# Splitting first loads, seams and the last norm of an encoder layer kernel, and holding GpSimd's sums back

## The chip, the cores and the metric

The kernel runs on one core of one Trainium2 chip. The metric is device time in microseconds (us) of one launch. The core's engines are TensorE (PE; weight loads are shown as PEld), VectorE (DVE), ScalarE (ACT), GpSimd (POOL) and SyncE (SP), which issues the DMA transfers. They run side by side and wait for each other through counting semaphores.

## What is computed

One encoder layer in float32, width D = 1024, for 1024 + 256 = 1280 tokens (two sequences, laid side by side), in these steps:

```
z      = x @ w_in                                    # 1024 wide, into heads, rwkv parts, gates
o_att  = attention(q, k, v)                          # 8 query heads, 2 key/value heads
o_rw   = (groupnorm(wkv scan both ways) + bonus) * g # 16 heads of 64
merged = gate0 * (o_rw @ w_proj_rwkv) + gate1 * (o_att @ w_proj_attn)
h      = layernorm(ALPHA * x + merged @ w_out)       # over the 1024 columns
ff     = square(relu(h @ w_ff1)) @ w_ff2             # 4096 wide
y      = layernorm(ALPHA * h + ff)
```

## The kernel before

Activations are kept transposed: 8 tiles of 128 rows (columns of the model), each with 1280 tokens along the free dimension. Six stages follow each other, with a barrier of all engines between them (class `Stage`): attention, scaled, gate, state, merge, tail. Inside a stage each engine has its own written-out list of instructions, and only semaphores order them across engines. The change touches three places.

*Attention stage, start.* SP first loads the weights of head 0 (512 KB), then the eight tiles of x (640 KB each), then the rest. TensorE's `head(0)` runs k outermost: for each of eight tiles k it multiplies spans of 512, 512 and 256 tokens into three PSUM banks, so that it can start with the first tile. A float32 matmul appears as two passes of weight load and product.

*Merge stage.* It has 16 blocks i, of 24 products each. Blocks 0 to 7 multiply the attention output (in xT); blocks 8 to 15 multiply the recurrent output oR. During blocks 0 to 7 the group norm of oR is done beside: ACT squares, TensorE sums over heads, ACT takes Ln and Exp, DVE scales, adds the bonus and multiplies by the gate g, one step of `normed` for each tile i and span j, 24 in all. Block 8 waits for all 24 on TensorE. `gating` on DVE multiplies a block's result by its gate (semaphore `gated`) and from block 8 adds it to merged (`added`), in one operation each over 1280 tokens. SP reloads xT with x when block 7 is done, and the weights of block 9 follow it in the queue.

*Tail stage.* The tokens are in two halves (H = 640), each of two quarters (Q = 320). Products come in pairs n, each a seven-product scheme in place of eight: sums of weight blocks (DVE, `add_weights`, semaphore `s_done`) times sums of token blocks. For the out projection the token sums of half 0 are DVE's (`wide_sums`, `tm_done`), those of half 1 GpSimd's (`other_half`, `tn_done`), both at the start of the stage; those of half 1 are first used by pair 4. A pair's products raise z1 to z7, and DVE's gathers out of PSUM raise e1 to e7. `p1(n+1)` is the first product of the next pair.

Each of the four norms (two layer norms, two halves; the last is N2H1) runs in steps: GpSimd adds the eight rows of 640 tokens (`totals`, four calls p = 0 to 3, the last two adds behind the last pair), TensorE multiplies the total by ones (means), DVE subtracts (`centre`), ACT squares, the squares are summed, TensorE multiplies by ones (variance), ACT takes Ln and Exp (`root`), a multiply by rstd (`scale`), ACT's `affine` (gain and bias), SP stores. For N2H1 TensorE sums the squares of all eight rows itself (16 products), and DVE scales all eight rows.

## Time and profile before

| | us |
|---|---|
| median of 3 runs | 3328.92 (3327.21 to 3331.74) |
| the profiled execution | 3333.99 |
| its span | 3332.2 |
| TensorE busy in it | 3216.5 (97%) |
| DVE, ACT, GpSimd busy | 1787.0, 1040.4, 136.9 |
| GpSimd's four sums at the start of the tail stage | 2176.05 to 2190.9 |
| last product of the last pair ends | 3297.4 |

The span runs from the first to the last recorded instruction; times in rows are from its start. Busy time adds the durations of an engine's instructions. Matmuls are pipelined and their ends are modelled, so a busy TensorE is not one at its peak. In a row, the bracket holds the engine's idle time before it and what ended it.

### The profile page before, as it was taken

What the parts mean: (1) busy time and instruction counts of PE and PEld (TensorE: products, weight loads), DVE (VectorE), ACT (ScalarE), POOL (GpSimd) and SP (SyncE); (2) the same over time, 40 slices, a digit from 0 to 9 for tenths busy, and PEclk for the clock granted to TensorE, in tenths of its full rate; (3) what the DMA queues carried; (4) which work ended last, traced back from release to release, by engine and by line L of the source; (5) the groups of instructions that cost most, each with busy time, mean ns of one, the idle gap of its engine ahead of it and who ended that gap; (6) DMA issues with size and microseconds to landing.
All of it is one profiled execution on the core that took longest, in us unless ns stands there. A gap on an engine that the chain in (4) does not pass through costs nothing. (4 is left out here: it accounts for less than half of the span.)

```text
span 3332.2 us, 59858 instructions
## 1 busy us (share of the span) xinstructions
PE 3216.5 (97%) x25992; PEld 2047.2 (61%) x25992; DVE 1787.0 (54%) x2925; ACT 1040.4 (31%) x1590; POOL 136.9 (4%) x90
## 2 busy tenths in 40 slices
PE   9999999999999999989999999989999999999997
PEld 4564565554555555577787554567666666666665
DVE  2337763677767579056566232155645446545455
ACT  2336652334334124333443452002321111221111
POOL 0000000000000000000000000025200000200001
PEclk9999999999999999999999999999999999999998
DMA  3221111334534424265564223212112112122111
GB/s 139 57 73 33 45 33 49 122 123 148 184 124 129 177 95 151 100 193 167 170 171 126 84 88 140 82 38 76 58 61 75 68 64 82 57 95 82 63 64 57
DMA packets 218534, 328.53 MB, mean 99 GB/s; under 512 B 55456, under 2 KB 176544, under 8 KB 213152
## 3 DMA queue, kind: packets, MB, share of 16 engines
q1 hardware_dynamic: 218272, 324.69, 29.9%
q8 instruction: 207, 3.39, 0.4%
q14 instruction: 55, 0.45, 0.0%
HBM read 221.74 MB, written 96.34 MB: 95 GB/s over the span
## 5 line engine op out<-in xcount | busy, mean ns | idle before, releaser
L641 PE MATMUL ra_ps<-xT,ring 128*128 128x512 f32 (+1 forms) x1152 | 429.8, 526 | 0.0
L1817 PE MATMUL tl_ps<-merged,pool 128*128 128x320 f32 x1440 | 406.1, 434 | 4.6 <-PEq L108 3.9
L1817 PEld LDWEIGHTS tl_ps<-merged,pool 128*128 128x128 f32 x1440 | 274.6, 191 | 121.0 <-issue 7.5
L641 PEld LDWEIGHTS ra_ps<-xT,ring 128*128 128x128 f32 x1152 | 214.5, 190 | 198.8 <-issue 189.1
L2069 DVE TENSOR_TENSOR oR<-tl_ps,oR 128x320 f32<-128x320 f32 x416 | 202.3, 490 | 152.7 <-PE tl_ps L1817 149.9
L1091 PE MATMUL rg_ps<-xT,ring 128*128 128x512 f32 (+1 forms) x720 | 267.5, 527 | 3.3 <-PEq L108 3.3
L1817 PE MATMUL tl_ps<-tl_Th,pool 128*128 128x320 f32 x720 | 205.5, 437 | 6.5 <-DVE xT L2067 6.5
L1902 ACT ACTIVATE ring<-tl_ps 128x320 f32<-128x320 f32 x96 | 42.0, 437 | 533.7 <-PE tl_ps L1817 533.7
L1091 PEld LDWEIGHTS rg_ps<-xT,ring 128*128 128x128 f32 x720 | 135.6, 192 | 115.4 <-issue 109.9
L2075 DVE TENSOR_TENSOR merged<-tl_ps,ring 128x320 f32<-128x320 f32 x96 | 47.2, 492 | 256.0 <-PE tl_ps L1817 140.5
L1817 PE MATMUL tl_ps<-xT,pool 128*128 128x320 f32 x640 | 182.7, 432 | 0.0
L1817 PEld LDWEIGHTS tl_ps<-tl_Th,pool 128*128 128x128 f32 x720 | 138.4, 192 | 64.9 <-issue 9.1
L1817 PE MATMUL tl_ps<-merged,tl_sums 128*128 128x320 f32 x544 | 161.8, 437 | 5.8 <-DVE oR L2067 3.3
L1297 PE MATMUL rc_ps<-pool 64*128 64x192 f32 x1280 | 153.3, 356 | 6.7 <-DVE rc_ps L1498 3.5
L303 PE MATMUL at_ps<-xT,ring 128*128 128x512 f32 (+1 forms) x432 | 159.1, 521 | 0.0
L1817 PEld LDWEIGHTS tl_ps<-xT,pool 128*128 128x128 f32 x640 | 121.7, 190 | 50.6
L1449 DVE TENSOR_TENSOR rc_SC<-rc_ps,cst 128x512 f32<-128x512 f32 x160 | 110.4, 690 | 71.1 <-PE rc_ps L1297 71.1
L1594 PE MATMUL mg_ps<-xT,ring 128*128 128x512 f32 (+1 forms) x384 | 144.5, 530 | 1.9 <-PEq L108 1.9
L328 PE MATMUL at_ps<-at_qk 128*128 128x512 f32 (+1 forms) x288 | 135.8, 594 | 8.3 <-ACT at_p L395 7.9
L1594 PE MATMUL mg_ps<-oR,ring 128*128 128x512 f32 (+1 forms) x384 | 139.4, 526 | 2.9 <-DVE oR L1647 2.9
L340 PE MATMUL at_ps<-at_turned,at_v 32*128 32x256 f32 x2176 | 137.0, 386 | 4.0 <-DVE at_ot L479 4.0
L340 PEld LDWEIGHTS at_ps<-at_turned,at_v 32*128 32x128 f32 x2176 | 108.4, 185 | 49.0 <-issue 43.4
(243 smaller groups left out, 4730.3 us busy)
## 6 DMA issues: line engine op xcount, KB each, us to landing
pool<-ub SPq DMA_DIRECT2D x320, 160.0 KB, 2.8
ub<-ra_ub SPq DMA_DIRECT2D x32, 1280.0 KB, 5.3
pool<-in_w_ff SPq DMA_DIRECT2D x32, 1024.0 KB, 4.8
pool<-in_w_ff SPq DMA_DIRECT2D x64, 512.0 KB, 3.5
ring<-in_w_in SPq DMA_DIRECT2D x39, 512.0 KB, 3.6
xT<-in_xT SPq DMA_DIRECT2D x16, 640.0 KB, 8.2
ub<-ra_v SPq DMA_DIRECT2D x16, 640.0 KB, 6.5
mg_gate<-gates SPq DMA_DIRECT2D x16, 640.0 KB, 3.9
```

The source lines that it names most:

```text
L303: last = pe.matmul(ps[:, z_bank(i) + j, 0:n], w[:, i % 3, 128 * k:128 * k + 128], xT[:, k, t0:t0 + n], start=(k == 0), stop=(k == KT - 1))
L328: last = pe.matmul(ps[:, 2 * (t % 2) + b // 512, 0:n], qk[:, h, t0:t0 + 128], qk[:, QH + h // (QH // KVH), k0 + b:k0 + b + n], start=True, ...
L340: last = pe.matmul(ps[:, 4 + i, 0:256], values_of(g, i, j), pT[g % 2][32 * i:32 * i + 32, j].rearrange("p t q -> p (t q)"), start=(j == 0) ...
L641: last = pe.matmul(ps[:, bank + j, 0:n], w[c][:, 128 * i:128 * i + 128], xT[:, i, t0:t0 + n], start=(i == 0), stop=(i == KT - 1))
L1091: last = pe.matmul(ps[:, 3 * (b % 2) + j, 0:n], w[b % 3][:, 128 * i:128 * i + 128], xT[:, i, t0:t0 + n], start=(i == 0), stop=(i == KT - 1))
L1297: last = pe.matmul(ps[:, 4 + 2 * (q % 2) + h, 192 * j:192 * j + 192], x[rows, 2 * q + j, CH:3 * CH], x[rows, 2 * q + j, 3 * CH:6 * CH], st ...
L1449: dve.tensor_tensor(SC[g % 2][:, 2 * q:2 * q + 2, :, :], score_view(ps, q, 0, 2 * CH), cst[:, at:at + 128].unsqueeze(1).unsqueeze(1).broad ...
L1594: last = pe.matmul(ps[:, 3 * (i % 2) + j, 0:n], w[i % 2][:, 128 * k:128 * k + 128], src[:, k, t0:t0 + n], start=(k == 0), stop=(k == KT - 1))
L1817: last = pe.matmul(bank(n, b), lhs(k), rhs(k), start=(fresh and k == 0), stop=(k == d - 1), skip_group_check=True)
L1902: act.activation(cp[n % 2][:, c, :], bank(n, b), ACT.Copy).then_inc(done, 1)
L2069: dve.tensor_tensor(y, bank(n, b), y, ALU.add).then_inc(done, 1)
L2075: dve.tensor_tensor(hidden(n, i, j), bank(n, b), cp[n % 2][:, c, :], ALU.add).then_inc(done, 1)
```

## The change

Five edits are made. (1) The first weights and the first x tile are loaded in two pieces each, the first 128 columns of w and the first 512 tokens of x first, with a semaphore of their own; TensorE waits for the pieces as it comes to them. (2) Block 8 of the merge waits for the last tile's `normed` steps only before its k = 7 products. (3) The last block's gating runs span by span. (4) GpSimd's `other_half` waits until DVE's four token sums and the weight sums of pairs 0 and 1 are done. (5) In the last norm DVE adds the last two rows to the totals by quarters; the squares are added in pairs of rows, two pairs by GpSimd and two by DVE, so that TensorE has 8 products in place of 16; GpSimd scales rows 6 and 7 and applies gain and bias to them; and the stores go in the order 0, 1, 2, 6, 3, 4, 7, 5.

```diff
@@ attention_stage, SP
-            load(0)
-            for k in range(KT):
+            sp.dma_start(w[:, 0, 0:128], hbm["w_in"][B_Q + HEADS[0]][:, 0:128]).then_inc(first_ready, 16)
+            sp.dma_start(xT[:, 0, 0:512], hbm["xT"][0:128, 0:512]).then_inc(first_ready, 16)
+            sp.dma_start(xT[:, 0, 512:T], hbm["xT"][0:128, 512:T]).then_inc(x_ready[0], 16)
+            sp.dma_start(w[:, 0, 128:D], hbm["w_in"][B_Q + HEADS[0]][:, 128:D]).then_inc(w_ready[0], 16)
+            for k in range(1, KT):
@@ attention_stage, TensorE, head(0)
-                        pe.wait_ge(x_ready[k], 16)
+                        if k == 0:
+                            pe.wait_ge(first_ready, 32)
+                        else:
+                            pe.wait_ge(x_ready[k], 16)
+                        if k == 1:
+                            pe.wait_ge(w_ready[0], 16)
                         for j, (t0, n) in enumerate(SPANS):
+                            if k == 0 and j == 1:
+                                pe.wait_ge(x_ready[0], 16)
@@ merge_stage, TensorE
                 if i == KT:
-                    pe.wait_ge(normed, 3 * KT)
+                    pe.wait_ge(normed, 3 * KT - 3)
...
                     for k in range(KT):
+                        if i == KT and k == KT - 1:
+                            pe.wait_ge(normed, 3 * KT - 2 + j)
...
-                    if j == 2:
+                    if i == 2 * KT - 1:
+                        last.then_inc(z_part, 1)
+                    elif j == 2:
                         last.then_inc(z_ready, 1)
@@ merge_stage, DVE
-            for i in range(KT, 2 * KT):
+            for i in range(KT, 2 * KT - 1):
                 gating(i)
+            i = 2 * KT - 1
+            dve.wait_ge(gate_ready[i % 2], 16 * (i // 2) + 16)
+            for j, (t0, n) in enumerate(SPANS):
+                g, m = gate[i % 2][:, t0:t0 + n], merged[:, KT - 1, t0:t0 + n]
+                dve.wait_ge(z_part, j + 1)
+                dve.tensor_tensor(g, ps[:, 3 * (i % 2) + j, 0:n], g, ALU.mult).then_inc(gated_part, 1)
+                dve.wait_ge(gated_part, j + 1)
+                dve.tensor_tensor(m, m, g, ALU.add).then_inc(added, 1)
@@ tail_stage, SP
-            store(N2H1)
+            for k in (0, 1, 2, 6, 3, 4, 7, 5):
+                if k < 6:
+                    sp.wait_ge(normed, 8 * N2H1 + k + 1)
+                else:
+                    sp.wait_ge(gp_normed, k - 5)
+                sp.dma_start(hbm["y"][128 * k:128 * k + 128, H:T], rows(N2H1, k)).then_inc(stored, 16)
@@ tail_stage, TensorE, variance of N2H1
-            for k in range(KT):
-                pe.wait_ge(sq_done, 8 * N2H1 + k + 1)
+            for k in range(0, KT, 2):
+                pe.wait_ge((gp_sums, dve_sums)[k // 4], k % 4 // 2 + 1)
                 for j in range(2):
...
@@ tail_stage, ACT
-            for k in range(KT):
+            for k in range(6):
                 affine(N2H1, k)
@@ tail_stage, GpSimd
-                    if 0 <= p < 4:
+                    if 0 <= p < (3 if q == N2H1 else 4):
...
+            gp.wait_ge(tm_done, 4)
+            gp.wait_ge(s_done, 8)
             for which in (1, 2, 3, 4):
                 other_half(which)
...
+            for k in (0, 2):
+                gp.wait_ge(sq_done, 8 * N2H1 + k + 2)
+                gp.tensor_tensor(squares(N2H1, k), squares(N2H1, k), squares(N2H1, k + 1), ALU.add).then_inc(gp_sums, 1)
+            gp.wait_ge(r_done, N2H1 + 1)
+            for k in (6, 7):
+                gp.wait_ge(centred, 8 * N2H1 + k + 1)
+                gp.tensor_tensor(rows(N2H1, k), rows(N2H1, k), rstd[:, :], ALU.mult).then_inc(gp_scaled, 1)
+                gp.wait_ge(gp_scaled, k - 5)
+                gp.tensor_scalar(rows(N2H1, k), rows(N2H1, k), glob[:, G_L2G + k:G_L2G + k + 1], glob[:, G_L2B + k:G_L2B + k + 1],
+                                 ALU.mult, ALU.add).then_inc(gp_normed, 1)
@@ tail_stage, DVE
+            def last_total(k, j, ready, done):
+                n, t = PAIRS_N - 1, tot[:, Q * j:Q * j + Q]
+                if k == 3:
+                    dve.wait_ge(tot_part, 6 * N2H1 + 5)
+                else:
+                    dve.wait_ge(end_part, (1, 2)[j])
+                dve.wait_ge(ready, n + 1)
+                dve.tensor_tensor(t, t, rows(N2H1, k)[:, Q * j:Q * j + Q], ALU.add).then_inc(done, 1)
...                                  # behind gather e3 of the last pair
+                if n == PAIRS_N - 1:
+                    last_total(3, 0, e2, end_part)
+                    last_total(3, 1, e3, end_part)
+                    last_total(7, 1, e7, tot_part)
...                                  # behind gather e4
+                if n == PAIRS_N - 1:
+                    dve.wait_ge(tot_part, 6 * N2H1 + 6)
+                    last_total(7, 0, e4, tot_done)
...
             for k in range(KT):
                 centre(N2H1, k)
-            for k in range(KT):
+            for k in (4, 6):
+                dve.wait_ge(sq_done, 8 * N2H1 + k + 2)
+                dve.tensor_tensor(squares(N2H1, k), squares(N2H1, k), squares(N2H1, k + 1), ALU.add).then_inc(dve_sums, 1)
+            for k in range(6):
                 scale(N2H1, k)
```

## Rows read from the trace of the kernel before

**Rows 1.** The page's engine line: busy us (share of the span) xinstructions.

```profile
PE 3216.5 (97%) x25992; PEld 2047.2 (61%) x25992; DVE 1787.0 (54%) x2925; ACT 1040.4 (31%) x1590; POOL 136.9 (4%) x90
```

**Rows 2.** Timeline of the start: start us, us, engine, line, operation [idle before <-releaser].

```profile
6.21 19.21 PE L297 MATMUL at_ps<-xT,ring 128*128 128x512 f32 x48 [6.21 <-DMA xT<-in_xT]
8.90 0.34 PEld L297 LDWEIGHTS at_ps<-xT,ring 128*128 128x128 f32 x1 [0.52 <-issue]
```

**Rows 3.** Timeline of the merge stage, end of block 7 and block 8.

```profile
2029.06 0.70 PE L1578 MATMUL mg_ps<-mg_gd,mg_wg 128*128 128x256 f32 x2 [0.28 <-DVE oR L1647]
...
2032.67 35.66 PE L1594 MATMUL mg_ps<-oR,ring 128*128 128x512 f32 x93 [2.91 <-DVE oR L1647]
...
2051.83 1.49 DVE L1632 TENSOR_TENSOR mg_gate<-mg_ps,mg_gate 128x1280 f32<-128x1280 f32 x1 [17.91 <-PE mg_ps L1594]
```

**Rows 4.** Timeline of the last norm.

```profile
3298.19 3.14 POOL L1992 TENSOR_TENSOR ring<-ring,oR 128x640 f32<-128x640 f32 x2 [3.30 <-DVE oR L2069]
3301.38 2.50 PE L1888 MATMUL tl_ps<-ring,cst 128*128 128x320 f32 x4 [3.94 <-POOL ring L1992]
...
3303.91 5.94 DVE L2079 TENSOR_TENSOR oR<-oR,tl_ps 128x640 f32<-128x640 f32 x8 [5.95 <-PE tl_ps L1888]
3304.77 5.86 ACT L1925 ACTIVATE xT<-oR 128x640 f32<-128x640 f32 x8 [65.82 <-DVE oR L2079]
...
3305.65 11.25 PE L1895 MATMUL tl_ps<-xT,cst 128*128 128x320 f32 x32 [1.77 <-ACT xT L1925]
...
3320.67 6.60 ACT L1930 ACTIVATE oR<-oR,glob 128x640 f32<-128x640 f32 x8 [0.89 <-DVE oR L2083]
```

**Rows 5.** Windows of the last norm: stretch, length, busy us by engine, PEclk, DMA share, GB/s.

```profile
3305.60:3310.50 4.90, 4.85 (x9) 3.21 (x10) 4.25 (x6) 4.90 (x7) 0.00 (x0) 0.50 0.01 3
...
3319.80:3327.30 7.50, 0.00 (x0) 0.00 (x0) 5.97 (x8) 6.60 (x8) 0.00 (x0) 0.56 0.65 260
```

**Rows 6.** Timeline of the attention stage, a shorter stall of TensorE and what follows.

```profile
215.09 0.70 PE L286 MATMUL at_ps<-at_turned,cst 128*128 128x256 f32 x2 [2.47 <-ACT at_turned L372]
...
215.62 6.64 PE L318 MATMUL at_ps<-ring,xT 128*128 128x256 f32 x30
```

**Rows 7.** Windows of the start of the program.

```profile
0.00:3.00 3.00, 0.00 (x0) 0.00 (x0) 0.00 (x0) 0.00 (x0) 0.20 (x4) 1.00 0.28 76
3.00:6.00 3.00, 0.00 (x0) 0.00 (x0) 0.00 (x0) 0.00 (x0) 0.00 (x0) 1.00 1.03 417
```

**Rows 8.** One line in a stretch, 2025 to 2060: weight loads of the merge stage.

```profile
L1543 SPq DMA_DIRECT2D ring<-in_w_merge x2: 328/442/556, 2032.3 to 2051.8; - x2
...
DMA to landing us min/median/max: 3.6/8.0/12.4
```

**Rows 9.** Timeline of the merge stage's end and the tail stage's start.

```profile
2172.14 1.49 DVE L1632 TENSOR_TENSOR mg_gate<-mg_ps,mg_gate 128x1280 f32<-128x1280 f32 x1 [14.17 <-PE mg_ps L1594]
2173.66 1.49 DVE L1634 TENSOR_TENSOR merged<-merged,mg_gate 128x1280 f32<-128x1280 f32 x1
...
2175.98 0.69 DVE L2024 TENSOR_TENSOR pool<-pool 128x512 f32<-128x512 f32 x1 [0.83 <-PEq L108]
...
2176.05 3.37 POOL L1969 TENSOR_TENSOR oR<-merged 128x1280 f32<-128x1280 f32 x1 [754.45 <-POOLq L108]
2176.59 4.18 DVE L2037 TENSOR_TENSOR tl_Th<-merged 128x1280 f32<-128x1280 f32 x1
...
2188.07 0.47 DVE L2067 SCALAR_TENSOR_TENSOR xT<-xT,tl_ps 128x320 f32<-128x320 f32 x1
...
2188.69 9.49 PE L1817 MATMUL tl_ps<-tl_Th,pool 128*128 128x320 f32 x24 [6.46 <-DVE xT L2067]
```

**Rows 10.** Timeline of the tail stage's second pair, DVE and one product of TensorE.

```profile
2201.38 0.69 DVE L2032 TENSOR_TENSOR tl_sums<-pool,tl_sums 128x512 f32<-128x512 f32 x1
...
2209.39 0.68 DVE L2024 TENSOR_TENSOR pool<-pool 128x512 f32<-128x512 f32 x1
...
2215.24 2.32 PE L1817 MATMUL tl_ps<-merged,tl_sums 128*128 128x320 f32 x8
```

**Rows 11.** One line of the program, in the gate stage: GpSimd's copies, duration ns.

```profile
L1141 POOL COPY pool<-cst x2: 609/611/613, 1121.8 to 1122.3; 128x512 f32<-128x512 f32 x2
```

More of the change, by code:

```diff
@@ L173, in attention_stage @@
         w_ready = st.sems("w_ready0 w_ready1 w_ready2")
-        c_ready, tab_ready, om, zr_ready = st.sems("c_ready tab_ready om zr_ready")
+        c_ready, tab_ready, om, zr_ready, first_ready = st.sems("c_ready tab_ready om zr_ready first_ready")
         z_ready, sq_done, zq_done, stat_ready, ln_done, rt_done, zn_done, cos_done, sin_done, head_done = st.sems(
@@ L288, in head @@
             def head(i):
-                pe.wait_ge(w_ready[i % 3], 16 * (i // 3) + 16)
+                if i:
+                    pe.wait_ge(w_ready[i % 3], 16 * (i // 3) + 16)
                 if i >= 2:
@@ L1533, in merge_stage @@
         w_ready, gate_ready = (st.sems(f"{n}0 {n}1") for n in ("w_ready", "gate_ready"))
-        low_ready, bon_ready, x_back = st.sems("low_ready bon_ready x_back")
+        low_ready, bon_ready, x_back, z_part, gated_part = st.sems("low_ready bon_ready x_back z_part gated_part")
         z_ready, gated, added, sq_done, var_ready, ln_done, rt_done, g_ready, scaled, biased, normed = st.sems(
@@ L1665, in tail_stage @@
         e1, e2, e3, e4, e5, e6, e7 = st.sems("e1 e2 e3 e4 e5 e6 e7")
-        tn_done = st.sems("tn_done")[0]
+        tn_done, end_part = st.sems("tn_done end_part")
+        gp_sums, dve_sums, gp_scaled, gp_normed = st.sems("gp_sums dve_sums gp_scaled gp_normed")
         s_done, tm_done, th_done, tx_done, relu_done, h_done = st.sems("s_done tm_done th_done tx_done relu_done h_done")
@@ L1891, in _ @@
             pe.wait_ge(e4, PAIRS_N)
-            for k in range(KT):
-                pe.wait_ge(sq_done, 8 * N2H1 + k + 1)
+            for k in range(0, KT, 2):
+                pe.wait_ge((gp_sums, dve_sums)[k // 4], k % 4 // 2 + 1)
                 for j in range(2):
-                    last = pe.matmul(ps[:, j, 0:Q], ones, squares(N2H1, k)[:, Q * j:Q * j + Q], start=(k == 0), stop=(k == KT - 1))
+                    last = pe.matmul(ps[:, j, 0:Q], ones, squares(N2H1, k)[:, Q * j:Q * j + Q], start=(k == 0), stop=(k == KT - 2))
             last.then_inc(var_ready, 1)
```

## The prediction

> **What bounds the kernel now.** I read the page's engine line first, then the timeline of each stretch that an edit touches, for the idle time in the brackets of TensorE's rows, then windows of it for the granted clock and the DMA rate. TensorE is busy 97% of the span [rows 1], so only two things can give time: a stall of TensorE, or a stretch where it runs at 1.2 GHz in place of 2.4. A weight load takes 0.19 us at the one and 0.34 us at the other, with 0.24 or 0.52 us of pause behind 512-column passes (the slow kind stands in [rows 2]). After a stall of 2.91 us a block takes 2 us too long (worked out in B, [rows 3]); after one of 3.94 us the granted clock is 0.50 [rows 4, 5]; after one of 2.47 us passes of 256 columns still come every 0.22 us, full speed [rows 6]. So a stall removed pays itself and about 2 us of slow clock behind it. The change touches four places that rows show as not covered by TensorE: the first 6.21 us, the middle and the end of the merge stage with the start of the tail, and the last 35 us. Elsewhere it does nothing, so I add up the four.
>
> **A, first load.** Before: 512 KB of weights and 640 KB of x (1.18 MB) must land before the first pass at 6.21 [rows 2]. By 3.00 us 76 GB/s x 3 us = 0.23 MB have come, then 0.417 MB per us [rows 7], so 1.18 MB are in at 5.28, and 0.93 us pass until TensorE starts. After: 64 + 256 KB = 0.328 MB, in at 3.24, start at 4.2: 2.0 less. The split adds two issues of about half a us on SP's queue, ahead of x1 to x7; each of these needs 1.57 us to flow, so the queue is not late. Supply: the rest of x0 arrives at about 5.1 (needed at 5.9, after two slow passes of 0.34 + 0.52 us), the rest of w at 6.2 and x1 at 7.8 (needed at 8.4); a later k costs TensorE 2.15 us and the link 1.57, so no wait comes back. The slow first 4.4 us only move. Bounds: 0 (small rows flow badly, or a later wait absorbs the lead) to 2.3. I take **-2.0**.
>
> **B, middle seam.** At i = 8 TensorE waits for all 24 steps of `normed`: its last piece runs at 2029.06 and block 8 starts at 2032.67 [rows 3]. After, only the k = 7 product of each span waits, and the first comes 6.9 us into the block, when the last `normed` (2032.5) is done or, for span 0, long done. Block 8 can start at about 2029.6: 3.1. Besides, block 8 took 2051.83 - 2032.67 = 19.16 us, where a block at full rate takes 14.17 + 1.49 + 0.03 + 1.49 = 17.18 (DVE's idle time and its two operations fill one block [rows 9]); with no stall, that 1.98 goes too. What is late next: the weights of block 9 lie behind the reload of xT. They come 12.4 us after their issue at 2032.3 [rows 8], at 2044.7, and would be needed at 2029.6 + 17.2 = 2046.8; 2.1 us to spare. Bounds 3.1 (slow clock stays) to 5.1. **-5.1**.
>
> **C, end of merge.** Before: DVE works 1280 columns twice after the last pass, 2172.14 to 2175.15, and the tail's first instructions run 0.83 later [rows 9]. After: spans 0 and 1 are done under TensorE; behind it lie 256 columns twice. The nearest row is the 1.49 for 1280 columns: a fifth is 0.3 and with a start cost 0.42 each. DVE ends near 2173.0 in place of 2175.15: **-2.15**; the tail starts at S = 2173.8. TensorE's stall falls from 3.9 us (2172.1 to 2176.0) to 1.75, below the 2.47 that did no harm [rows 6], so the first eight products should run at 2.4 GHz.
>
> **D, sums at the tail's start.** Before, DVE and GpSimd alternate. DVE's token sum, 1.49 us alone (L1634, same shape, [rows 9]), takes 4.18 behind a GpSimd sum that began at 2176.05 and took 3.37. So e1 ends only at 2188.54, and the three products behind it at 2188.69 + 9.49 = 2198.18: S + 22.2 with S = 2175.98. After, GpSimd waits for DVE. DVE starts an operation 0.08 before the recorded end of the last, so a weight sum is 0.61 and a token sum 1.41: 2 + 2 of them 4.04, e1 at 4.5, TensorE goes on at 4.6 (its first two products end at 4.3), at full speed. Then e1's 0.40, another 4.04, e2 0.40, e6 0.47: 9.35. The product that waits ends 2.32 later [rows 10], at S + 11.7. Gain 10.5.
> The price: GpSimd's four sums (3.37, less about 0.6 of waiting: 2.8 each, at most 3.1) now begin after `s_done` 8, at 2202.07 in old times [rows 10], = T. They hold until T + 12.9. DVE meets them at L2024 of the next pair, T + 7.3 [rows 10]: it waits for the third sum (to 9.25), runs 0.69, GpSimd's fourth takes 2.8, the second weight sum ends at 13.45, and the gather e5 behind it at 13.9. Queued behind them are also e7, e1 and the next two weight sums, all with slack. TensorE needs e5 for z3 at 2215.24 = T + 13.17: it waits 0.7. `tn_done` is wanted first in pair 4, some 45 us on; GpSimd's first row total follows at T + 12.9 and nobody is near. Bounds 0 to 5 (both weight sums meet a whole sum each and z3 waits for all). D is **-9.8**.
>
> **E, last norm.** *Totals.* Before: GpSimd adds two rows, 3298.19 to 3301.33, mean matmuls from 3301.38, 2.50 us at half rate after a stall of 3.94 [rows 4]. After: DVE adds quarters, 320 columns, at about 0.48 us (its 1280 columns take 1.49). Three of them run behind e3 (ends 3296.9) and before e4, which they push from 3297.5 to 3298.1; the last ends at 3299.15. Means start at 3299.2; the stall is then 1.75 us, so full rate, 1.25: mean at M = 3300.45, not 3303.88. -3.4 (bounds -2.2, half rate, to -3.5).
> *Variance.* Before: 16 products in pairs, M to 3316.9 = 13.0. After: DVE centres end at M + 5.97 as before, squares at M + 6.75, four pair sums (GpSimd from M + 2.45 and M + 4.05, 1.53 each; DVE, 0.75, until M + 7.55), 8 products. Centring reads one operand from PSUM; the gather e1, which does too, took its plain 0.47 us beside GpSimd's fourth sum [rows 9], so these do not collide. TensorE stands 4.0 us until the first pair sum, so it restarts at 1.2 GHz: 1.07 us a product. The stretch after 3305.6 stayed at half clock for 4.9 us [rows 5]; I take 4.5: 4.2 products at 1.07, 3.8 at 0.53, from M + 4.05 to M + 10.8. TensorE, not DVE's sums, is the last: 2.2 less (bounds 1.5 to 3.2; halving the products gains little since they start late and slow). ACT's roots, 2.9 us, are unchanged.
> *Scale and affine.* From R = 3320.67 - 0.89 (rstd ready) DVE scaled eight rows, each 0.75 behind the last as in centring, and ACT followed until R + 7.5 [rows 4], while stores left at 260 GB/s [rows 5]; the end of the span is 4.9 later, R + 12.4. After, DVE has six and GpSimd two rows. Both scalings read two SBUF operands, which take turns as the sums of [rows 9] do; I give the affine a turn of its own like them: s0 | g6 | s1 | a6 | s2 | g7 | s3 | a7 | s4 s5 = 6 x 0.75 + 2 x 1.53 + 2 x a. GpSimd's affine (one input) has no row; the nearest is its one-input copy, 0.611 us for 512 columns [rows 11], so 0.76 for 640; at most the two-input 1.53. The sixth scaling ends at R + 9.1, its ACT row (0.92) at R + 10.1, the end 4.9 later, R + 15.0: **+2.6** (bounds 0, no collision, to +4.2). Here the edit costs.
> The rows show turns only between two-input operations; if the affine ran beside DVE, the end would be 1.5 earlier, +1.1. The Trainium skill, "SBUF — State Buffer", section "Who interferes with whom", says that a DVE instruction with two SBUF inputs contends with any GpSimd instruction that reads SBUF; by it the affine blocks too and +2.6 stands. The Trainium skill, "GPSIMD Engine Reference", "Elementwise — side-by-side cycle accounting", gives 1.8 cycles an element at 1.2 GHz for its best one-input loop: an estimate of 0.96 us for the affine, and +3.0 by it. The trace of before shows neither.
> E: -3.4 - 2.2 + 2.6 = **-3.0**.
>
> **Sum.** -2.0 - 5.1 - 2.15 - 9.8 - 3.0 = -22.05. The profiled execution took 3333.99 (span 3332.2 and 1.8 around it), so 3311.9 under the profiler. The median of the runs is 3328.92, 5.1 lower; the same difference gives **3306.9**.
>
> **Rivals.**
> 1. *The lock costs more (0.15).* GpSimd's sums delay z3 by up to 5 us, and the last scalings cost +4.2. For: the turns in [rows 9]. Against: DVE has 7 us free of two-input work after T. -22.05 + 4.3 + 1.6 = -16.15: 3312.8.
> 2. *The clock does not come back (0.10).* A stall of 1.75 us is enough for 1.2 GHz at the tail's start (about 1.0) and at the means (1.2), and block 8 runs slowly all the same (2.0). For: 1.75 was never seen clean next to other short stalls. Against: [rows 6]. -17.85: 3311.1. The border between 2.47 and 2.91 us is only known from single stalls.
> 3. *The early start does not arrive (0.06).* The split load gives nothing, or a DMA wait absorbs it: 3308.9. This is the change not doing what it says in one part.
> 4. *Slower (0.02).* GpSimd's late sums and the three adds of row totals behind them each catch a two-input operation that TensorE has no slack for, and each stall also costs the clock: 4 x (2.8 + 2.0) + 3 x (1.53 + 2.0) = 29.8 against the 22.05: +7.7, 3336.6. It decides once more than five of the seven hit. Against: DVE has only four weight sums in a pair of 15 us, and two of them fall behind GpSimd's last.
>
> **Chances.** Forecast 0.67, with its own range 3303 to 3310; rivals as given. The range for 8 in 10 takes in rival 1 nearly: 3301.5 to 3312.5. The low end is the sum with E's end at 0 and no wait in D (-3.3), and 2 us by which runs differ. Within 0.2% (6.7 us, about what can be told from no change) or slower needs rival 4: faster 0.97, same 0.01, slower 0.02.
>
> **What would show it.** First pass at 4.2, not 6.2 (A). No idle time ahead of L1594 near 2027 and block 8 in 17.2 (B). TensorE's stall at the stage change 1.75, with loads of 0.19 (C). The first pair's third product ends 11.7 after the tail starts; GpSimd's sums begin about 16 after it, with one long L2024 and a stall near 0.7 before z3 (D). Mean matmuls 1.25 long, variance 10.8 after them, long DVE scalings of about 2.2 at the end, and R to the end 15.0 rather than 12.4 (E). I am wrong if the last part gains, if block 9 waits for weights, or if the lead of A is gone by the end of the attention stage.

## The result and the profile after

The changed kernel takes 3305.62 us (median of 6 runs, 3301.87 to 3308.13); the kernel before, run beside it, 3328.41 (6 runs, 3323.09 to 3333.9). The ratio is 0.9929, 95% interval 0.9917 to 0.994: 22.8 us faster, where the prediction said 22.05. In a later set of runs (e9, e10 below) the same two kernels gave 0.9940 (0.9926 to 0.9954). The profiled execution took 3303.59, its span 3301.8.

The engine line of the page, to be laid beside [rows 1]:

```profile
PE 3201.6 (97%) x25976; PEld 2035.7 (62%) x25976; DVE 1785.4 (54%) x2933; ACT 1038.7 (31%) x1588; POOL 142.7 (4%) x94
```

TensorE has 16 passes fewer and is busy 14.9 us less, yet the span is 30.4 shorter. The rest, 15.5 us, is time in which TensorE stood. Where it stood is told by the stretches that the prediction named. Each is measured from one event to another in both profiled executions:

| stretch | before | after | difference | predicted |
|---|---|---|---|---|
| A, program start to head 1's first product | 25.26 | 24.05 | -1.2 | -2.0 |
| B, start of the seam's last short product to the end of block 8 | 22.8 | 17.9 | -4.85 | -5.1 |
| C, TensorE's stall at the end of the merge stage | 3.89 | 1.75 | -2.14 | -2.15 |
| D, tail start to the first product of pair 8 | 129.70 | 119.47 | -10.23 | -9.8 |
| E, last main product to the end of the span | 34.8 | 30.9 | -3.9 | -3.0 |
| sum | | | -22.3 | -22.05 |

The end of D is the first product of pair 8, where the feed-forward part begins (the first row is the kernel before, the second the changed one):

```profile
2305.68 0.70 PE L1817 MATMUL tl_ps<-xT,pool 128*128 128x320 f32 x2
2280.76 0.97 PE L1846 MATMUL tl_ps<-xT,pool 128*128 128x320 f32 x3
```

The sum of the stretches agrees with the medians. The single profiled pair differs by 8.1 more, and nearly all of that lies where nothing was changed: the state stage took 430.1 us before and 423.4 after (-6.7), the first half of the merge stage -1.6, the tail from pair 8 to the last main product -1.6, the scaled and gate stages +1.9. Behind the last three stands the granted clock: each holds a stall that both kernels have, behind which the clock fell for longer in one of the two executions than in the other, or only in one of them (table in the last section). A window of the state stage, in the columns of [rows 5], for the changed kernel, and one for a repeat of before (e9):

```profile
1420.70:1844.00 423.30, 392.90 (x12672) 334.82 (x12672) 256.47 (x559) 167.68 (x361) 0.61 (x1) 0.99 0.56 162
```

```profile
1424.00:1862.00 438.00, 397.83 (x12672) 338.06 (x12672) 256.99 (x559) 168.54 (x361) 0.61 (x1) 0.99 0.56 156
```

The same 12,672 passes take 423 to 438 us at the same granted clock of 0.99. In all thirteen profiled executions of this study the stage lay between 423.4 and 442.7 at a clock of 0.98 to 0.99, whichever edits were in. So one execution's total can't judge an edit of 2 us here; stretches can, and everything below goes by them.

**The start.** Timeline, as [rows 2], and the window of 3 to 6 us, as [rows 7]:

```profile
3.90 4.09 PE L308 MATMUL at_ps<-xT,ring 128*128 128x512 f32 x6 [3.90 <-DMA xT<-in_xT]
8.90 15.31 PE L308 MATMUL at_ps<-xT,ring 128*128 128x512 f32 x42 [0.92 <-DMA xT<-in_xT]
24.05 6.17 PE L314 MATMUL at_ps<-xT,ring 128*128 128x512 f32 x14
```

```profile
3.00:6.00 3.00, 2.10 (x3) 1.02 (x4) 0.00 (x0) 0.00 (x0) 0.00 (x0) 1.00 0.96 308
```

TensorE starts 2.3 us earlier, at 3.90. But between 3 and 6 us the queues move 308 GB/s where they moved 417, and the first row's six passes are followed by 0.92 us of idle time for x1. Head 1 starts 1.2 earlier: about half of the lead is lost. The lower rate is no accident of this execution: it was 298 to 364 GB/s in all ten profiled executions with split loads, and 417 to 423 in the three with whole ones.

**The merge's seam.** As [rows 3]:

```profile
2021.35 0.70 PE L1589 MATMUL mg_ps<-mg_gd,mg_wg 128*128 128x256 f32 x2 [0.27 <-DVE oR L1662]
...
2021.88 30.65 PE L1607 MATMUL mg_ps<-oR,ring 128*128 128x512 f32 x79
...
2039.27 1.49 DVE L1647 TENSOR_TENSOR mg_gate<-mg_ps,mg_gate 128x1280 f32<-128x1280 f32 x1 [13.07 <-PE mg_ps L1607]
```

The first row is the last short product of the group norm, the last row is DVE taking up block 8's result. Block 8 starts 0.5 us after the start of the short product instead of 3.6, and its result is taken up 17.4 later instead of 19.16: full rate throughout. No wait for the weights of block 9 shows.

**The stage change and the tail's start.** As [rows 9]. S is the first product's start, here 2161.30.

```profile
2159.58 0.42 DVE L1671 TENSOR_TENSOR mg_gate<-mg_ps,mg_gate 128x256 f32<-128x256 f32 x1 [2.04 <-PE mg_ps L1607]
2160.04 0.42 DVE L1673 TENSOR_TENSOR merged<-merged,mg_gate 128x256 f32<-128x256 f32 x1
2161.30 4.54 PE L1846 MATMUL tl_ps<-merged,pool 128*128 128x320 f32 x16 [1.75 <-PEq L108]
2161.90 1.48 DVE L2078 TENSOR_TENSOR tl_Th<-merged 128x1280 f32<-128x1280 f32 x1
...
2170.74 2.39 PE L1846 MATMUL tl_ps<-tl_Th,pool 128*128 128x320 f32 x8 [0.26 <-DVE xT L2108]
2172.97 4.47 PE L1846 MATMUL tl_ps<-merged,pool 128*128 128x320 f32 x16
```

The last gating works on 256 columns, 0.42 us each time; the stall is 1.75 us and the 16 passes behind it take 4.54, which is full speed (6.24 in the kernel before). The token sum takes 1.48 instead of 4.18. Pair 0 ends and pair 1's first product starts at 2172.97, S + 11.67 (before: S + 22.03). GpSimd's sums now come 15.9 us after S, and here they meet DVE's next weight sums, as foreseen:

```profile
2177.17 2.89 POOL L1998 TENSOR_TENSOR oR<-merged 128x1280 f32<-128x1280 f32 x1 [754.49 <-DVE tl_sums L2073]
...
2184.34 2.08 DVE L2065 TENSOR_TENSOR pool<-pool 128x512 f32<-128x512 f32 x1
...
2186.45 3.26 DVE L2068 TENSOR_TENSOR pool<-pool 128x512 f32<-128x512 f32 x1
...
2190.25 2.39 PE L1846 MATMUL tl_ps<-merged,tl_sums 128*128 128x320 f32 x8
```

Two weight sums that take 0.69 alone take 2.08 and 3.26. The gather behind them (2189.63, 0.47 us) is done in time, though: the product that needs it follows without an idle time worth a bracket.

**The last norm.** As [rows 4] and [rows 5]:

```profile
3270.30 1.55 DVE L2126 TENSOR_TENSOR ring<-ring,oR 128x320 f32<-128x320 f32 x3
...
3272.39 0.49 DVE L2126 TENSOR_TENSOR ring<-ring,oR 128x320 f32<-128x320 f32 x1
...
3272.94 1.63 PE L1917 MATMUL tl_ps<-ring,cst 128*128 128x320 f32 x4 [2.00 <-DVE ring L2126]
3274.61 5.94 DVE L2130 TENSOR_TENSOR oR<-oR,tl_ps 128x640 f32<-128x640 f32 x8 [1.72 <-PE tl_ps L1917]
...
3278.70 7.21 PE L1924 MATMUL tl_ps<-xT,cst 128*128 128x320 f32 x16 [4.13 <-POOL xT L2049]
...
3288.83 7.70 DVE L2134 TENSOR_TENSOR oR<-oR,pool 128x640 f32<-128x640 f32 x6 [6.66 <-ACT pool L1950]
3288.87 2.17 POOL L2053 TENSOR_TENSOR oR<-oR,pool 128x640 f32<-128x640 f32 x1 [8.80 <-ACT pool L1950]
...
3291.15 2.63 POOL L2055 TENSOR_SCALAR oR<-oR,glob 128x640 f32<-128x640 f32 x1
...
3293.75 2.09 POOL L2053 TENSOR_TENSOR oR<-oR,pool 128x640 f32<-128x640 f32 x1
...
3295.95 1.32 POOL L2055 TENSOR_SCALAR oR<-oR,glob 128x640 f32<-128x640 f32 x1
```

```profile
3278.70:3282.90 4.20, 4.20 (x8) 2.83 (x9) 3.40 (x5) 3.90 (x5) 1.37 (x1) 0.50 0.02 6
```

DVE's quarter sums shorten TensorE's stall from 3.94 to 2.00 us. The means take 1.63 us, neither 2.50 nor the 1.24 of four passes among others at full rate. The variance products start after 4.13 us of idle time at a granted clock of 0.50. DVE's six scalings take 7.70 us where eight took 5.97.

### The profile page after: what moved, and what is told of

It reads as the page before. It is cut to its first block and busy times, and to the rows that moved or that the text cites. A ratio compares the mean times of both kernels' runs of the same rounds, so it can differ in the third digit from the quotient of the medians.

```text
span 3301.8 us, 59842 instructions
## 1 busy us (share of the span) xinstructions
PE 3201.6 (97%) x25976; PEld 2035.7 (62%) x25976; DVE 1785.4 (54%) x2933; ACT 1038.7 (31%) x1588; POOL 142.7 (4%) x94
```

## The experiments

Each stretch is read from one profiled execution of the kernel. The kernels e5, e6, e8 and e11 also carry another order of the first loads, which is shown at e5. Of e1 to e8 there is one time each, which can't judge an edit of 2 us: the kernel before, run once beside each set, took 3336.32 (e1 to e4) and 3346.14 (e5 to e8), and the state stage alone moves by more than most edits do.

| run | time, us | its state stage, us |
|---|---|---|
| e1 | 3324.56 | 439.9 |
| e2 | 3326.62 | 433.2 |
| e3 | 3320.27 | 439.4 |
| e4 | 3325.42 | 441.3 |
| e5 | 3326.14 | 439.1 |
| e6 | 3326.30 | 441.9 |
| e7 | 3330.31 | 442.5 |
| e8 | 3319.84 | 442.7 |

**e1: the first loads whole again.** Edit (1) undone, all else as changed.

```diff
-            sp.dma_start(w[:, 0, 0:128], ...).then_inc(first_ready, 16)
...
-            for k in range(1, KT):
+            load(0)
+            for k in range(KT):
```

> The kernel after, with the first load as before (w of head 0 whole, then x0 whole); the other edits stay. Theory (the split gives TensorE a lead that nothing takes back inside the attention stage): first product at 6.2 rather than 3.9 us, second head (L314 in the kernel after) starts at 25.3 rather than 24.05, so 1.2 later, and the products of the values start 1.2 later too. Rival (the lead is lost in a later wait, the attention stage is bound by something else): the values' start is within 0.2 us of the kernel after. The later stages (scaled, gate, state) differed by up to 7 us between the two profiled executions although nothing in them changed; if that comes from the early start, the state stage here takes the 430.1 us of the kernel before; if it is run to run, it takes any length between 423 and 431.

The first product starts at 6.22 and head 1 at 26.05 (25.3 was expected). The two executions of the kernel before (before, e9) have 25.26 and 26.04 there, so the mean of three is 25.8. Six with edit (1) in this order (the changed kernel, e2, e3, e4, e7, e10) have 24.05, 24.08, 25.06, 26.73, 24.25 and 23.41, mean 24.6. The edit is worth 1.2 us on average, from three and six executions that spread by 0.8 and 3.3, and in one execution (e4) it was worth nothing. The attention stage's last product moves alike: it ends at 518.9 on average with the whole load and at 517.6 with the split one, so the lead that is left lasts to the end of the stage. The tail stretches stay as in the changed kernel (pair 1 starts at S + 11.67). The start is thus a gain of its own. The state stage took 439.9 us, neither the 430.1 of the one reading nor within the 423 to 431 of the other: it varies by more than the expectation allowed.

**e2: GpSimd's sums at once.**

```diff
-            gp.wait_ge(tm_done, 4)
-            gp.wait_ge(s_done, 8)
```

> The kernel after, with GpSimd's sums of the other token half starting at once, as in the kernel before; all else stays. Theory (DVE and GpSimd take turns whenever both read two SBUF operands): DVE's first token sum takes about 4.2 us rather than 1.48, the second pair's first product (p1 of pair 1) starts about 10 us later counted from the tail stage's start (22 rather than 11.7), and the long stall makes TensorE restart at 1.2 GHz. Rival (most of the gain at this place came from the stage starting at full clock, not from the sums): the distance grows by no more than 3 us.

```profile
2173.28 4.54 PE L1846 MATMUL tl_ps<-merged,pool 128*128 128x320 f32 x16 [1.75 <-PEq L108]
...
2173.35 3.37 POOL L1998 TENSOR_TENSOR oR<-merged 128x1280 f32<-128x1280 f32 x1 [748.80 <-POOLq L108]
2173.89 4.18 DVE L2076 TENSOR_TENSOR tl_Th<-merged 128x1280 f32<-128x1280 f32 x1
...
2185.98 6.76 PE L1846 MATMUL tl_ps<-tl_Th,pool 128*128 128x320 f32 x16 [8.15 <-DVE xT L2106]
```

All of the stretch comes back: pair 1 starts at S + 22.02 (S + 11.67 with the waits, S + 22.03 before), and TensorE stands 8.15 us. The first product of pair 8 starts at S + 129.69 or 129.70 in the three executions without the waits (before, e2, e9) and at S + 119.46 to 119.49 in the ten with them. This kernel keeps edit (3), and its first 16 passes run at full rate as in the changed one. So the gain doesn't come from the clock with which the stage starts; it is the alternation of two engines' sums, and two waits are worth 10.35 us.

**e3: the last two rows by DVE and ACT again.**

```diff
-            for k in (0, 1, 2, 6, 3, 4, 7, 5):
...
+            store(N2H1)
-            for k in range(6):
+            for k in range(KT):          # affine and scale
-            gp.wait_ge(r_done, N2H1 + 1)
-            for k in (6, 7):
...
```

> The kernel after, with all eight rows of the last norm scaled by DVE and given gain and bias by ACT, stores in order 0 to 7; totals and pair sums of squares stay. Theory (GpSimd's two rows cost more in turns than they save): from the end of Exp to the end of the span 12.4 us, as before, against 13.0 in the kernel after, so 0.6 shorter, and DVE's eight scalings 0.75 us apart. Rival (sharing helps, and the longer distance comes from something else, such as the order of the stores): 13.0 or longer.

```profile
3306.04 5.97 DVE L2122 TENSOR_TENSOR oR<-oR,pool 128x640 f32<-128x640 f32 x8 [6.51 <-ACT pool L1945]
```

Eight scalings take 5.97 again, and from R (rstd ready) to the end it is 12.5 us. Five executions without GpSimd's rows lie at 12.4 to 12.8, eight with them at 13.0 to 13.8. This part of edit (5) costs 0.6 us or a little more. e3 also stores in the order 0 to 7 again, so the 0.6 is the net of GpSimd's rows and the order of the stores; no run parts the two.

**e4: the clock kept through the variance.** Seven extra products, whose result nothing uses, between the means and the variance.

```diff
+            for _ in range(7):
+                pe.matmul(ps[:, 2, 0:Q], ones, tot[:, 0:Q], start=True, stop=True)
```

> The kernel after, with seven products of ones by the row totals, into an unused PSUM bank, between the mean products and the first product of the variance; their results are not used. Theory (in the last norm the variance is bound by TensorE's clock, which falls in the 4.1 us wait for the first pair sum): no stall over 1 us there, variance products at 2.4 GHz, and from the mean to the end of the variance about 8.9 us rather than 11.35 (DVE's last pair sum at 7.6, then two products), so 2.4 us shorter to the end. Rival (the pair sums themselves bound it): within 0.5 us of 11.35.

```profile
3298.16 5.28 PE L1922 MATMUL tl_ps<-ring,cst 128*128 128x320 f32 x14
...
3303.27 4.47 PE L1926 MATMUL tl_ps<-xT,cst 128*128 128x320 f32 x16
```

The 16 passes of the variance take 4.47 us, full rate, and it ends 9.38 after the mean instead of 11.34. The half clock had cost 2.0 us. The seven are too many: they started at half clock and ran about 0.9 us past the first pair sum; the end came 0.5 later than the 8.9 expected.

**e5: the middle seam waits for all steps.** Edit (2) undone, and the loads in a new order: the second 128 columns of w, then x1, then the rest of w.

```diff
-                    pe.wait_ge(normed, 3 * KT - 3)
+                    pe.wait_ge(normed, 3 * KT)
...
-                        if i == KT and k == KT - 1:
-                            pe.wait_ge(normed, 3 * KT - 2 + j)
```

```diff
-            sp.dma_start(w[:, 0, 128:D], ...).then_inc(w_ready[0], 16)
-            for k in range(1, KT):
+            sp.dma_start(w[:, 0, 128:256], ...).then_inc(first_rest, 16)
+            sp.dma_start(xT[:, 1, :], hbm["xT"][128:256, :]).then_inc(x_ready[1], 16)
+            sp.dma_start(w[:, 0, 256:D], ...).then_inc(w_ready[0], 16)
+            for k in range(2, KT):
```

> The kernel after, with block 8 of the merge waiting for all 24 steps of normed again; and with another order of the first loads: w columns 0 to 127, x0 tokens 0 to 511, the rest of x0, w columns 128 to 255, x1, the rest of w, x2 and on. Seam: theory (a stall of 3 us plus a block at half clock): block 8 starts 3.3 us after the last piece rather than 0.2, and block 9 starts 19.0 us after it rather than 17.2. Rival (the half clock of the kernel before was chance, the clock is not tied to this stall): 17.2. First load: the split kernel's x1 came at 8.6 to 9.9 us, a stall of 0.7 to 2.0, because the small pieces flow at about 310 GB/s and all of w lies before x1; with 0.39 MB of w behind x1 it should land about 1 us earlier, at 7.6 to 8.9, and the second head start by 24.0. Rival (the small rows themselves slow all that follows): x1 lands no earlier, second head at 24.05 to 26.7 as in the four looks at the split load so far.

```profile
2042.56 21.70 PE L1609 MATMUL mg_ps<-oR,ring 128*128 128x512 f32 x54 [2.91 <-DVE oR L1664]
```

```profile
2044.00:2047.40 3.40, 3.40 (x6) 1.27 (x5) 0.00 (x0) 0.00 (x0) 0.00 (x0) 0.58 1.03 429
```

The stall of 2.91 is back, and from block 8's start to the use of its result (2061.72) it is 19.16 us again. The window 1.4 us into the block shows a granted clock of 0.58. The new load order showed no stall for x1 here and head 1 at 23.79, as expected; but the same order gave 26.21 in e6, with a stall of 0.53, and 24.02 and 22.86 in e8 and e11. The mean of the four, 24.2, against 24.6 for six with the first order, does not show that the order helps.

**e6: the same seam, its stall filled.** As e5, with three products of unused result in the stall.

```diff
+                    for _ in range(3):
+                        pe.matmul(ps[:, 0, 0:512], w[0][:, 0:128], oR[:, 0, 0:512], start=True, stop=True)
+                    pe.wait_ge(normed, 3 * KT)
```

> As e5_seam_waits_for_all, with three products of 512 tokens in front of the wait for all normed steps, written where block 8 writes afterwards; their results are overwritten. Theory (the half clock comes from TensorE standing still, not from what it waits for): block 8 starts about 3.3 us after the last piece of block 7, as in e5, but runs its 24 products in 17.2 us, not 19.0. Rival (the loads that run at the same time, the reload of xT, slow block 8): 19.0. First load: as expected for e5.

```profile
2041.42 2.74 PE L1607 MATMUL mg_ps<-oR,ring 128*128 128x512 f32 x6
...
2044.39 20.03 PE L1612 MATMUL mg_ps<-oR,ring 128*128 128x512 f32 x54 [0.24 <-DVE oR L1667]
2061.89 1.49 DVE L1652 TENSOR_TENSOR mg_gate<-mg_ps,mg_gate 128x1280 f32<-128x1280 f32 x1 [16.15 <-PE mg_ps L1612]
```

Block 8 starts as late as in e5, but takes 17.5 us instead of 19.16: 54 passes in 20.03 against 21.70. Of edit (2)'s 4.8 us, 1.7 are the clock and 3.1 the wait itself. The expectation of 17.2 for the block was 0.3 too low: even without any stall it takes 17.39. The two terms of step B are each shown. The loads run here as in e5, so they are not what slows the block.

**e7: sixteen variance products again.** The pair sums of squares removed.

```diff
-            for k in range(0, KT, 2):
-                pe.wait_ge((gp_sums, dve_sums)[k // 4], k % 4 // 2 + 1)
+            for k in range(KT):
+                pe.wait_ge(sq_done, 8 * N2H1 + k + 1)
...
-            for k in (0, 2):             # GpSimd's pair sums
...
-            for k in (4, 6):             # DVE's pair sums
...
```

> The kernel after, without the pair sums of squares: TensorE multiplies all eight squared rows by ones, 16 products, as before; DVE's totals by quarters and the shared last rows stay. Theory (the clock decides): the wait ahead of the first product is 1.7 us rather than 4.1; if TensorE is still at 2.4 GHz when it starts, 16 products keep pace with ACT's squares and end about 1.3 after the last of them, at 8.2 to 10.3 us behind the mean, so the pair sums cost 1 to 3 us. Rival (the pair sums help): with the clock down for the first 4 to 5 us the 16 products take until 12 to 13 us behind the mean, against 11.3 to 11.6 in the kernel after.

```profile
3297.32 1.34 PE L1917 MATMUL tl_ps<-ring,cst 128*128 128x320 f32 x4 [2.01 <-DVE ring L2123]
3300.44 11.83 PE L1924 MATMUL tl_ps<-xT,cst 128*128 128x320 f32 x32 [1.77 <-ACT xT L1954]
```

The variance ends 13.60 after the mean, against 11.1 to 11.6 with pair sums. My theory (starting with the first square would bring the clock back early and the pair sums be worth little) has fallen, and the rival was right: although TensorE stood only 1.77 us here and the means had run at full rate, the clock was at half from the first pass (granted clock 0.50 from 3300.4 to 3302.4), and the 32 passes from there on end 2.0 to 2.5 us later than the 16 that start later.

**e8: both places kept warm.** Three extra products before the means and five before the variance, results unused; last rows by DVE and ACT as in e3; the load order of e5.

```diff
+            for _ in range(3):
+                pe.matmul(ps[:, 2, 0:Q], ones, cst[:, 0:Q], start=True, stop=True)
...
+            for _ in range(5):
+                pe.matmul(ps[:, 2, 0:Q], ones, tot[:, 0:Q], start=True, stop=True)
```

> The kernel after, with three products of constants in the stall before the means and five of ones by totals before the variance (results unused), all eight last rows scaled by DVE and finished by ACT, and the load order of e5. Theory: means at 2.4 GHz, 3.2 us from the last main product to the mean rather than 3.4 to 3.8; variance 8.9 us rather than 11.3; last rows 12.4 rather than 13.0 to 13.8: about 3.5 us less from the last main product to the end than in the kernel after (30.9). Rival (the extra products delay the waited ones): less than 2 us gained, with the means or the first variance product starting later.

From the last main product to the mean 3.35 us (3.64 in the changed kernel), mean to variance 9.19 (11.34), R to the end 12.4 (13.0). The last norm takes 27.9 us in all, against 30.9 and, before, 34.8: 3.0 less, where 3.5 was expected.

**e9 and e10: both kernels again, unchanged, with five rounds each; e11: the kernel of e8, timed beside them.**

> The kernel before, once more, so that its stages can be compared with looks from other chips. Theory (the state stage, which nothing in the change touches, varies by itself): it takes some length between 423 and 443 us here, not the 430.1 of the first look, and the last norm, the seam and the tail's start take the lengths of the first look to 0.1 to 0.5 us: 3.3 + 19.0 at the seam, 22.0 from the tail's start to the second pair. Rival (the change moved the state stage): 430 within 1 us, while all kernels with the change in the same call lie elsewhere. Timed against itself: ratio 1.000 within its interval.

> The kernel after, once more, timed on the chip of e9. Theory (the gain is the sum of the five stretches, 21 to 23 us, whatever the chip): ratio to the kernel before 0.9930 to 0.9940. Rival (the gain depends on the chip; the single runs beside e1 to e8 showed the kernels with the change only 10 to 26 us faster than the kernel before): a ratio outside 0.991 to 0.996.

> The kernel of e8 (extra products before the means and before the variance, last rows by DVE and ACT, other order of the first loads), timed. Theory: 3.0 us less than the kernel after in the last norm and 0 to 1 at the start, so 3 to 4 us below e10 and a ratio to the kernel before of 0.9918 to 0.9930. Rival (at this size the state stage's own variation hides it): the interval of e11 overlaps that of e10 wholly and the medians lie within 1 us.

| kernel | median us | ratio to before | 95% interval |
|---|---|---|---|
| e9, before | 3345.46 | 1.0005 | 0.9996 to 1.0015 |
| e10, changed | 3322.45 | 0.9940 | 0.9926 to 0.9954 |
| e11 | 3315.93 | 0.9917 | 0.9905 to 0.9930 |

The kernel before, run beside all three, has a median of 3342.94, 14.5 us more than in the first set of runs. The ratio of the change moves only from 0.9929 to 0.9940. e9 and e10 repeat the stretches: pair 1 starts at S + 22.02 and S + 11.67, the stall ahead of block 8 is 2.91 us and gone, mean to variance 13.06 and 11.50, R to the end 12.5 and 13.0. In e11:

```profile
3284.17 1.78 PE L1914 MATMUL tl_ps<-cst 128*128 128x320 f32 x6
3286.34 1.34 PE L1918 MATMUL tl_ps<-ring,cst 128*128 128x320 f32 x4 [0.39 <-DVE ring L2122]
3287.52 2.85 PE L1923 MATMUL tl_ps<-ring,cst 128*128 128x320 f32 x10
...
3291.73 1.34 PE L1927 MATMUL tl_ps<-xT,cst 128*128 128x320 f32 x4 [1.35 <-POOL xT L2052]
3293.24 3.64 PE L1927 MATMUL tl_ps<-xT,cst 128*128 128x320 f32 x12 [0.17 <-POOL xT L2052]
```

Every row of it is at full rate. All five runs of e11 (3312.44 to 3318.84) lie below all five of e10 (3321.27 to 3325.24), though the intervals of the two ratios overlap a little, so that e11 beats the changed kernel is shown too. The medians differ by 6.5 us, more than the 3 to 4 expected. The last norm gives 2.7 of it (28.2 us here, 30.9 in e10) and the start may give 0.5 (head 1 at 22.86 and 23.41). Where the rest comes from is open; the mean granted clock was 0.993 to 0.995 in the five runs of e11 and 0.991 to 0.993 in those of e10.

## Why the prediction was right

**The total** was 3306.9 against 3305.62, in the range and in the likeliest case's own. It rests on D and B, which make up two thirds, and on them the experiments bear the mechanism out. That the total came within 0.3 us of the sum is luck: A fell short by 0.8 and B by 0.25, D and E gave 0.4 and 0.9 more, and these cancel. The step from the profiled execution to the median, a difference of 5.1 us taken over, had no ground either: the changed kernel's profiled execution lies 2.0 below its median. It did no harm, since it amounts to taking 22.05 from the median of before.

**A: term mis-sized, -1.2 in place of -2.0.** The supply was computed at 417 GB/s, the rate of whole loads. With small pieces in front, it is 308 between 3 and 6 us, x1 comes late (0.92 us of stall here; 0.49, 1.81 and 2.04 in three of the five other executions with this load order), and the lead melts. I had set x1 at 7.8 against a need at 8.4, 0.6 us to spare on one rate; it was needed at 8.0 and came at 8.9. The clock takes a share as well, which the sum left out: the slow weight loads of 0.34 us end with the 7th pass in the changed kernel and only with the 16th in e4 and e6, where head 1 started last (26.73 and 26.21).

**B: right in both terms.** The wait was to give 3.1 (e5 against the changed kernel: 3.1) and the clock 2.0 (e6 against e5: 1.7; a block at full rate takes 17.39, not 17.18).

**C: right** to 0.01 us, with the 0.42 for 256 columns, and the clock stays: behind the stall of 1.75 the first eight passes took 2.39 us in all eleven executions with edit (3). The reason given, that 2.47 us "did no harm" in [rows 6], does not hold. That row was one execution. Behind the same stall of 2.47 the clock fell in eight of thirteen, the repeat of the kernel before among them (window of e9, in the columns of [rows 5]):

```profile
215.90:219.90 4.00, 4.00 (x11) 3.23 (x12) 0.14 (x1) 3.51 (x4) 0.00 (x0) 0.57 0.01 4
```

The forecast was right here with a support that did not bear it; the same support failed in E.

**D: right, the price too high.** The first pair's third product was to end at S + 11.7, and pair 1 follows it at S + 11.67. The price of GpSimd's late sums was put at 0.7 and pair 8 shows 0.13 (10.36 gained at pair 1's start, 10.23 left at pair 8's). GpSimd's first three sums took 2.89 us each, and the third was done at T + 8.9, not 9.25, so the gather ended at T + 13.1, where T + 13.9 was foreseen and T + 13.2 needed. Rival 1 (up to 5 us here) did not come.

**E: right in sign and nearly in sum, -3.9 in place of -3.0, by errors that cancel.**
- The step "1.75 us, so full rate" did not hold. TensorE's stall was 2.00, since DVE's first three adds took 1.55 rather than 1.44, the gather behind them began at 3271.78 and the fourth add only at 3272.39, and the clock fell while the means ran, in most executions: in nine executions the means took 1.34 to 1.88 us after the same stall of 2.00 or 2.01, and 1.42 or more in seven of them. That is the mechanism of rival 2, at a price of up to 0.6 rather than 1.2. The term gave 2.8, not 3.4.
- The variance took 11.34, not 10.8: the slow weight loads went on for 5.4 us, where 4.5 had been taken over from [rows 5]. It gave 1.7, not 2.2. (The prediction's own terms, 4.2 x 1.07 + 3.8 x 0.53 from M + 4.05, end at M + 10.55 and not at 10.8, so the miss is 0.8.) e4 shows that the clock is the cause.
- The last rows cost 0.6, not 2.6. Two of its terms were off. One is the turn-taking. The two-input scalings did take turns: DVE's first rows lasted 2.16 beside GpSimd's 2.17. GpSimd's affine reads one SBUF tile and was recorded at 2.63 us, but DVE finished two scalings inside it, and the third waited for only about 0.5 us more than the 0.81 that it takes alone:

```profile
3289.57 2.16 DVE L2134 TENSOR_TENSOR oR<-oR,pool 128x640 f32<-128x640 f32 x1
...
3292.39 0.81 DVE L2134 TENSOR_TENSOR oR<-oR,pool 128x640 f32<-128x640 f32 x1
3293.12 1.33 DVE L2134 TENSOR_TENSOR oR<-oR,pool 128x640 f32<-128x640 f32 x1
3294.37 2.15 DVE L2134 TENSOR_TENSOR oR<-oR,pool 128x640 f32<-128x640 f32 x1
```

  Thus the sixth scaling ended at R + 7.7 instead of R + 9.1. The other term is the end: the span ended 4.3 us after the last ACT row where 4.9 had been carried over. That less was queued behind the last row, since the stores were spread out, is likely but not tested: with the same order of the stores it was 5.1 in e2 and 4.7 in e7.
  The Trainium skill, "SBUF — State Buffer", section "Who interferes with whom", says that a DVE instruction with two SBUF inputs contends with a GpSimd instruction that reads SBUF, and asks for no second input on GpSimd's side. The trace agrees that the affine waits for DVE and holds it up; it disagrees with the strict turns that I had made of it, since two scalings passed first.

Not settled: why the affine let two scalings by and the two-input sums never do, what makes the state stage of the same instructions take 423 or 442 us, and why e11 gains more than its stretches. No run here was aimed at these.

## What to carry to other kernels

Where DVE and GpSimd both ran operations with two SBUF operands here, they took turns (a DVE sum of 1.49 us took 4.18): delay the one whose result is needed later, and look where its work lands then. Here two waits gave 10 us, and the delayed sums collided again, in a place with slack. A stall of TensorE can have a second price in the granted clock behind it, so a known short stall is worth filling with products of no use, if these end before the wait does (1.7 us at the seam, 2 in the last norm). That one execution shows full rate behind a stall is no proof that the stall does no harm: look at the same place in several executions. Splitting a first load brings the start forward, but the margin of the next tile must be worked out at the rate of the split pieces.

## What the runs showed of the hardware

- The same stall before the same instructions left the clock at full rate in some executions and not in others. The time of the first eight passes behind it tells which:

| stall, us | where | executions | eight passes at full rate, us | eight passes otherwise, us |
|---|---|---|---|---|
| 1.75 | tail start, with edit (3) | 11 | 2.39 in 11 | none |
| 1.90 | merge start | 13 | 3.67 in 4 | 5.07 to 6.74 in 9 |
| 2.31 to 2.34 | scaled start | 13 | 3.67 in 5 | 5.37 in 8 |
| 2.47 | attention, [rows 6] | 13 | 1.99 in 5 | 3.21 to 3.62 in 8 |
| 2.91 | ahead of block 8 (before, e5, e9) | 3 | none | 5.15 to 5.37 in 3 |
| 3.24 to 3.26 | tail (2855.78 in the changed kernel) | 13 | 2.39 in 10 | 3.93 to 4.60 in 3 |
| 3.27 to 3.28 | gate start | 13 | 3.67 in 4 | 5.13 to 6.74 in 9 |

  So a single stall's length does not foretell the clock: 1.90 us cost it more often than 3.24. Behind the 4.13 us ahead of the variance products it was down in all seven executions that had that stall. At the scaled start it stayed up in just the five executions that leave the last two rows to DVE and ACT, an edit that acts some 2770 us later; no run explains that. The row behind the stall of 3.24, in the changed kernel:

```profile
2855.78 1.31 PE L1846 MATMUL tl_ps<-merged,tl_sums 128*128 128x320 f32 x4 [3.24 <-DVE oR L2108]
```

- GpSimd's gain and bias over 640 columns (one input tile) was recorded at 1.32 and 2.63 us, of which, by the ends of DVE's rows beside it, some 0.55 to 0.75 were its own work and the rest its wait for DVE; its two-input sum of 1280 columns took 2.89 alone.
- One stage of 12,672 passes varied between 423.4 and 442.7 us over thirteen executions at a granted clock of 0.98 to 0.99.
